# ScalarE's copies four slots behind TensorE's products in two tiles of an expert gather, with the query products and weight slots reordered

## What is computed

```python
def peer_ffn(h, wq, subkeys, u, v):
    ...
    q = (hf @ wq).reshape(T, PEER_HEADS, 2, D_HALF)
    s = jnp.einsum('thpd,pnd->thpn', q, subkeys, preferred_element_type=jnp.float32)
    top_s, top_i = lax.top_k(s, PEER_TOPK)
    cand = top_s[:, :, 0, :, None] + top_s[:, :, 1, None, :]
    best_s, best_j = lax.top_k(cand.reshape(T, PEER_HEADS, PEER_TOPK * PEER_TOPK), PEER_TOPK)
    ...
    expert = (i1 * N_KEYS + i2).reshape(T, PEER_HEADS * PEER_TOPK)
    gate = jax.nn.softmax(best_s, axis=-1).reshape(T, PEER_HEADS * PEER_TOPK).astype(h.dtype)
    ...
        uc = jnp.take(u, ec, axis=0)
        a = jnp.einsum('cd,ced->ce', hc, uc)
        act = jax.nn.gelu(a, approximate=False) * gc
        vc = jnp.take(v, ec, axis=0)
        return jnp.einsum('ce,ced->cd', act, vc)
```

## Time and profile before

| what | value |
|---|---|
| runs | 2619.51, 2631.34, 2619.8 us |
| median | 2619.8 us |
| span of the profiled execution, first to last instruction | 2623.7 us |
| PE / DVE / ACT / POOL busy | 81% / 51% / 30% / 40% of the span |
| tile 0 (window 170 to 556 us) | 386 us, 370 GB/s |
| tile 1 (556 to 990) | 434 us, 403 GB/s |
| tile 2 (990 to 1397) | 407 us, 368 GB/s |
| tile 3 (1397 to 1780) | 383 us, 371 GB/s |

### The profile page before, as it was taken

The page is one execution under the profiler, slowest core; times in us unless marked ns, Lnnn a source line. Parts: engine busy times, 40 slices in busy tenths (PEclk is TensorE's granted clock), DMA queues, the critical chain, the costliest instruction groups (busy, mean ns, idle before and its releaser), DMA issues. The chain is left out here.

```text
span 2623.7 us, 27482 instructions
## 1 busy us (share of the span) xinstructions
PE 2126.1 (81%) x8468; PEld 1120.2 (43%) x8468; DVE 1350.4 (51%) x2888; ACT 777.3 (30%) x2244; POOL 1040.3 (40%) x1107
## 2 busy tenths in 40 slices
PE   4887987676877879878877678868889998988997
PEld 2454543232333344434533223325645444655543
DVE  6756678774566475564685664432522223232222
ACT  2243332232324334353333334332410102321101
POOL 4036666576666556665556666650010000000000
PEclk9898989888988989999988889898889998988999
DMA  9749999999999999999999999993159996209996
GB/s 374 302 185 343 362 359 385 379 392 403 411 413 409 404 377 385 392 369 364 362 346 351 397 386 371 372 366 126 47 208 415 418 418 234 81 6 383 418 418 279
DMA packets 236992, 879.66 MB, mean 335 GB/s; under 512 B 23282, under 2 KB 29954, under 8 KB 214338
## 3 DMA queue, kind: packets, MB, share of 16 engines
q0 software_dynamic: 149488, 543.97, 54.1%
q1 hardware_dynamic: 87380, 334.23, 32.2%
HBM read 877.07 MB, written 1.05 MB: 335 GB/s over the span
## 5 line engine op out<-in xcount | busy, mean ns | idle before, releaser
L2212 DVE CUSTOM_DVE_ANT_0 arena<-arena,PS 128x1024 f32<-128x1024 f32 x512 | 625.0, 1221 | 484.6 <-DMA arena<-in_peer_u_dram,IDX 361.5
L933 POOL DMA_INDIRECT arena<-in_peer_v_dram,IDX x512 | 501.5, 979 | 423.0 <-PE PS L1531 233.8
L1531 PE MATMUL PS<-arena,JK 128*128 128x512 f32 x1024 | 526.5, 655 | 166.9 <-ACT JK L1089 96.3
L1531 PE MATMUL PS<-arena 128*128 128x512 f32 x1024 | 516.5, 643 | 147.2 <-issue 74.1
L930 POOL DMA_INDIRECT arena<-in_peer_u_dram,IDX x512 | 493.9, 965 | 308.8 <-issue 146.7
L1531 PEld LDWEIGHTS PS<-arena,JK 128*128 128x128 f32 x1024 | 201.5, 208 | 441.6 <-issue 393.9
L1531 PEld LDWEIGHTS PS<-arena 128*128 128x128 f32 x1024 | 197.9, 205 | 412.0 <-issue 382.4
L1076 ACT ACTIVATE ACTV<-DOT 128x1 f32<-128x1 f32 x512 | 102.0, 199 | 768.0 <-DVE DOT L2212 447.8
L1925 PE MATMUL PS<-arena,HT 128*64 128x256 f32 x2048 | 236.6, 384 | 19.8 <-DMA arena<-in_w_down_dram 13.3
L1925 PEld LDWEIGHTS PS<-arena,HT 128*64 128x64 f32 x2048 | 148.9, 137 | 98.4 <-DMA arena<-in_w_down_dram 22.8
L1084 ACT ACTIVATE GACT<-ACTV,GATE 128x1 f32<-128x1 f32 x512 | 150.8, 295 | 23.1 <-issue 2.8
(11 more groups left out here) (351 smaller groups left out, 1940.2 us busy)
## 6 DMA issues: line engine op xcount, KB each, us to landing
arena<-in_w_gate_dram SPq DMA_DIRECT2D x64, 1024.0 KB, 16.3
arena<-in_w_up_dram SPq DMA_DIRECT2D x64, 1024.0 KB, 18.4
arena<-in_w_down_dram SPq DMA_DIRECT2D x64, 1024.0 KB, 15.4
arena<-in_w_ada_dram SPq DMA_DIRECT2D x22, 2048.0 KB, 12.6
arena<-in_w_in_dram SPq DMA_DIRECT2D x11, 2048.0 KB, 17.9
arena<-in_peer_wq_dram SPq DMA_DIRECT2D x10, 2048.0 KB, 8.2
arena<-in_w_out_dram SPq DMA_DIRECT2D x6, 2048.0 KB, 10.1
arena<-in_peer_u_dram,IDX POOLq DMA_INDIRECT x512
```

The lines of the kernel that those rows point to most:

```text
L933: pool.indirect_dma_start(out=GV[b], out_offset=None, in_=v_rows, in_offset=off).then_inc(v_loaded[b], 16)
L1531: last = pe.matmul(PO[:, half, :], DIAG[n % DIAGS], GV[BUF[n]][:, half * 512:(half + 1) * 512], start=(j == 0), stop=False, skip_group_che ...
L2212: dve.tensor_tensor_reduce(GU[BUF[n]], GU[BUF[n]], HP[tt].rearrange("p b n -> p (b n)"), 1.0, 0.0, ALU.mult, ALU.add, DOT[:, s:s + 1]).the ...
```

## The change

The copies of ACT in tiles 0 and 2 (and the query copies of tile 3) move from one slot behind the product to four (`COPY`), PE's product with the subkeys from one or two slots behind the query product to five (`SCORE`), and ACT's copy of the scores from two or three to nine (`KEYED`). The tables move nearly all the steps of tile 2 and the query products and routing stages of tile 0:

- Tile 0: the query products start 4 to 9 slots later, the stages of (0, 2) at 41, 45, 49 and of (0, 3) at 53, 56, 59.
- Tile 2: four query products instead of five, at 20 (0, 3), 29 (0, 2), 99 (1, 0) and 109 (1, 1); the mixer's steps lie 3 to 20 slots later (the input products at 11, 14, 17, the attention's scores at 43, its output products at 76 and 83 instead of 60 and 63); three groups of routing stages instead of four.
- Tile 3: the product (1, 3) at 20 and the routing of (1, 1) at 5, 9, 13 come here from tile 2.
- The chunk ("wq", 1, 3) is loaded earlier and stays in its place until tile 3, so all the other chunks of that stretch share place 0. The order in which PE gives chunks back is therefore no longer that in which they are loaded, and `weight_chunks` counts it apart.
- Two buffers are placed elsewhere (`POOLT`, one part of `SS`), and POOL's transfers for the second block are issued at slot 52 of tile 3 instead of 40.

The loops of PE (`slots_beside_second_mixer` at L1610) and the second half of the `psum_jobs` hunk change by the same numbers as those shown, and are left out.

```diff
@@ -65,10 +65,11 @@
 LATE = (4, 5)
 BESIDE_TILE1 = (0, 1, 4, 5)
 
-WQ_AT = {10: (1, 0, 8), 19: (0, 2, 6), 31: (0, 3, 8), 41: (1, 1, 8), 51: (1, 2, 8), 67: (1, 3, 8)}
-ROUTE_AT = ([(0, 1, j) for j in (10, 13, 16)] + [(0, 2, j) for j in (37, 42, 47)] + [(0, 3, j) for j in (53, 57, 61)]
+COPY, SCORE, KEYED = 4, 5, 9
+WQ_AT = {14: (1, 0, 8), 26: (0, 2, 6), 36: (0, 3, 8), 48: (1, 1, 8), 60: (1, 2, 8), 72: (1, 3, 8)}
+ROUTE_AT = ([(0, 1, j) for j in (10, 13, 16)] + [(0, 2, j) for j in (41, 45, 49)] + [(0, 3, j) for j in (53, 56, 59)]
             + [(1, n // 3, 62 + 5 * n) for n in range(12)])
-GATES_AT = {16: 1, 47: 2, 61: 3, 117: 4}
+GATES_AT = {16: 1, 49: 2, 59: 3, 117: 4}
 
 SUM_AT = {(5 * n // 2 if n < 8 else 48 + 5 * (n - 8) // 2): n for n in range(24)}
 ADA_AT = {24: 0, 26: 1, 28: 2, 30: 3, 68: 4, 70: 5, 72: 6, 75: 7, 90: 8, 92: 9, 93: 10, 96: 11}
@@ -78,15 +79,16 @@
 FIRST_ROUTE_AT = {**{109 + 2 * n: (0, 0, n) for n in range(3)}, **{115 + 3 * n: (0, 1, n) for n in range(3)}}
 FIRST_GATES_AT = {114: 0, 122: 1}
 
-IN2_AT = {8: 0, 11: 1, 14: 2}
-OUT2_AT = {60: 0, 63: 1}
-NEXT_WQ_AT = {33: (0, 2, 4), 66: (0, 3, 4), 80: (1, 3, 4), 86: (1, 0, 4), 96: (1, 1, 4)}
-NEXT_ROUTE_AT = {**{45 + 2 * n: (0, 2, n) for n in range(3)}, **{78 + 2 * n: (0, 3, n) for n in range(3)},
-                 **{98 + 3 * n: (1, 0, n) for n in range(3)}, **{108 + 4 * n: (1, 1, n) for n in range(3)}}
-NEXT_GATES_AT = {49: 2, 82: 3, 104: 4, 116: 5}
-LAST_WQ_AT = {6: (1, 2, 8)}
-LAST_ROUTE_AT = {**{23 + 4 * n: (1, 2, n) for n in range(3)}, **{35 + 4 * n: (1, 3, n) for n in range(3)}}
-LAST_GATES_AT = {31: 6, 43: 7}
+IN2_AT = {11: 0, 14: 1, 17: 2}
+OUT2_AT = {76: 0, 83: 1}
+NEXT_WQ_AT = {20: (0, 3, 4), 29: (0, 2, 4), 99: (1, 0, 3), 109: (1, 1, 4)}
+NEXT_ROUTE_AT = {**{44 + 2 * n: (0, 2, n) for n in range(3)}, **{52 + 4 * n: (0, 3, n) for n in range(3)},
+                 **{113 + 3 * n: (1, 0, n) for n in range(3)}}
+NEXT_GATES_AT = {48: 2, 60: 3, 119: 4}
+LAST_WQ_AT = {6: (1, 2, 8), 20: (1, 3, 8)}
+LAST_ROUTE_AT = {**{5 + 4 * n: (1, 1, n) for n in range(3)}, **{25 + 4 * n: (1, 2, n) for n in range(3)},
+                 **{39 + 4 * n: (1, 3, n) for n in range(3)}}
+LAST_GATES_AT = {13: 5, 33: 6, 47: 7}
 REST_AT = 71
 QUERIES_AT = 80
 PIECES = 8
@@ -212,39 +214,39 @@
         if j - 2 in FIRST_WQ_DONE:
             add(("s", 1, *FIRST_WQ_DONE[j - 2]), "s", LATE)
     for j in range(SLOTS):
-        banks = BESIDE_TILE0 if j <= 76 else LATE
+        banks = BESIDE_TILE0 if j <= 94 else LATE
         if j == 6:
             halves("hT", 1, 1, banks)
         if j in IN2_AT:
             add(("in", 1, 1, IN2_AT[j]), "s", banks)
-        if j == 17:
+        if j == 24:
             add(("pool", 1, 1), "s", banks)
-        if j == 20:
+        if j == 29:
             add(("mix", 1, 1), "v", banks)
-        if j == 27:
...
@@ -334,8 +336,8 @@
     *[(("ada", 1, n), "v", n % 2 * 2) for n in range(4, 12)],
     (("out", 1, 0, 0), "p", 0), (("out", 1, 1, 0), "p", 2), (("wq", 1, 0, 0), "p", 0), (("wq", 1, 1, 0), "p", 2),
     (("in", 1, 0, 1), "p", 0), (("in", 1, 1, 1), "p", 2), (("in", 1, 2, 1), "p", 6),
-    (("wq", 1, 2, 0), "p", 0), (("out", 1, 0, 1), "p", 2), (("out", 1, 1, 1), "p", 0), (("wq", 1, 3), "p", 2),
-    (("wq", 1, 0, 1), "p", 0), (("wq", 1, 1, 1), "p", 2), (("wq", 1, 2, 1), "p", 0),
+    (("wq", 1, 2, 0), "p", 0), (("wq", 1, 3), "p", 2), (("out", 1, 0, 1), "p", 0), (("out", 1, 1, 1), "p", 0),
+    (("wq", 1, 0, 1), "p", 0), (("wq", 1, 1, 1), "p", 0), (("wq", 1, 2, 1), "p", 0),
 ]
 for _l in range(DEPTH):
     CHUNKS += [(("bin", _l, 3), "p", 0), (("bin", _l, 0), "p", 2), (("bin", _l, 1), "p", 1), (("bin", _l, 2), "p", 3),
@@ -349,12 +351,16 @@
 def weight_chunks():
 
 
-    chunks, count, last, kth = {}, {"v": 0, "p": 0}, {}, {}
+    given, nth = [name for name, _, _ in CHUNKS if name != ("wq", 1, NQ - 1)], {}
+    given.insert(given.index(("wq", 1, 2, 1)) + 1, ("wq", 1, NQ - 1))
+    users = {name: who for name, who, _ in CHUNKS}
+    for who in "vp":
+        nth.update({name: n for n, name in enumerate(name for name in given if users[name] == who)})
+    chunks, last, kth = {}, {}, {}
     for name, who, slot in CHUNKS:
         kth[slot] = kth.get(slot, 0) + 1
-        chunks[name] = (kth[slot], slot, who, count[who], last.get(slot))
+        chunks[name] = (kth[slot], slot, who, nth[name], last.get(slot))
         last[slot] = name
-        count[who] += 1
     return chunks
 
 
@@ -467,7 +473,7 @@
         QSQ = [[ap[:, 0:640] for ap in row] for row in S_A]
         S_A = [[parts(ap, NH) for ap in row] for row in S_A]
         PT_A = [[gv(7680, 1024), gv(8704, 1024)], [mod[:, 3584:4608], mod[:, 2560:3584]]]
-        POOLT = [[parts(ap[:, 0:512], 4) for ap in row] for row in PT_A]
+        POOLT = [[parts(ap[:, 0:512], 4) for ap in row] for row in (PT_A[0], [PT_A[1][0]] * TT)]
         PT_A = [[parts(ap, NH) for ap in row] for row in PT_A]
         SUBK = [parts(gv(10240, 256), 2), parts(mod[:, 4608:4864], 2)]
         MIXG = gv(10752, 1024)
@@ -478,7 +484,7 @@
         QTP = [mod[:, 10240:11264], mod[:, 2560:3584]]
         QTP = [[parts(ap[:, i * 512:(i + 1) * 512], 4) for i in range(2)] for ap in QTP]
         SS = [[[tt * 2048 + c * 512 for c in range(NQ)] for tt in range(TT)],
-              [[1536, 3584, 512, 6144], [6656, 7168, 7680, 8192]]]
+              [[1536, 3584, 512, 0], [6656, 7168, 7680, 8192]]]
         SS = [[[parts(mod[:, at:at + 512], 4) for at in row] for row in rows] for rows in SS]
         OH = gv(8704, 512).rearrange("p (h k c) -> p h k c", h=HQ, k=TOPK)
         CAND = parts(HR[:, 0, 0:512], HQ)
@@ -931,8 +937,8 @@
                         if PREV[n] is not None:
                             pool.wait_ge(expert_added, PREV[n] + 1)
                         pool.indirect_dma_start(out=GV[b], out_offset=None, in_=v_rows, in_offset=off).then_inc(v_loaded[b], 16)
-                        if l == DEPTH - 1 and tt == 1 and j == 40:
-                            arrived(pool, ("s", 1, 1, 2))
+                        if l == DEPTH - 1 and tt == 1 and j == 52:
+                            arrived(pool, ("s", 1, 1, 3))
                             params([(FINAL, row(final_norm_2, P))])
                             params_of_b(0)
 
@@ -1097,13 +1103,13 @@
                     slot_gate(l, 0, j)
                     if j - 1 == 5:
                         x_root(1)
-                    if j - 1 == 9:
+                    if j - COPY == 9:
                         transposed("h2T", l, 1)
                         h_to_psum(l, 1)
-                    if j - 1 in WQ_DONE:
-                        query(l, *WQ_DONE[j - 1])
-                    if j - 2 in WQ_DONE:
-                        keyed(l, *WQ_DONE[j - 2])
+                    if j - COPY in WQ_DONE:
+                        query(l, *WQ_DONE[j - COPY])
+                    if j - KEYED in WQ_DONE:
+                        keyed(l, *WQ_DONE[j - KEYED])
 
             def queries_of(l, tt):
                 copy_out(("fq", l, tt), FQT[:, :, tt * P:(tt + 1) * P], parts(bank(("fq", l, tt)), 4))
@@ -1153,34 +1159,34 @@
                 for j in range(SLOTS):
                     if j == 4:
                         x_root(1)
-                    if j == 23:
+                    if j == 25:
                         head_root(1)
-                    if j == 38:
+                    if j == 50:
                         head_exps(l, 1)
-                    if j == 56:
+                    if j == 68:
                         y_root(1)
-                    if j == 72:
+                    if j == 91:
                         x_root(1)
                     if j - 2 in NEXT_GATES_AT:
                         gate_exp(l, NEXT_GATES_AT[j - 2])
                     slot_gate(l, 0, j)
-                    if j - 1 == 6:
+                    if j - COPY == 6:
                         transposed("hT", l, 1)
-                    if j - 1 in IN2_AT:
-                        projected(l, 1, IN2_AT[j - 1])
-                    if j - 1 == 17:
+                    if j - COPY in IN2_AT:
+                        projected(l, 1, IN2_AT[j - COPY])
+                    if j - KEYED in NEXT_WQ_DONE:
+                        keyed(l, *NEXT_WQ_DONE[j - KEYED])
+                    if j - COPY in NEXT_WQ_DONE:
+                        query(l, *NEXT_WQ_DONE[j - COPY])
+                    if j - COPY == 24:
                         pooled(l, 1)
-                    if j - 1 == 27:
+                    if j - COPY == 33:
                         heads_transposed(l, 1)
-                    if j - 1 in NEXT_WQ_DONE:
-                        query(l, *NEXT_WQ_DONE[j - 1])
-                    if j - 3 in NEXT_WQ_DONE:
-                        keyed(l, *NEXT_WQ_DONE[j - 3])
-                    if j - 1 == 42:
+                    if j - COPY == 54:
                         probs_transposed(l, 1)
-                    if j - 1 == 58:
+                    if j - COPY == 71:
```

(36 more changed lines are left out.)

43 lines of the change are left out of this document (22 added, 21 removed).

## The result

The changed kernel takes 2641.8 us (median of 20 runs, 2629.2 to 2652.0), the kernel before 2631.0 us (median of 20, 2608.5 to 2648.7). The ratio is 1.0043, with a 95% interval of 1.0026 to 1.0059: slower by 0.3 to 0.6%. The middle, 0.43%, lies just under the 0.5% that the prediction took as no change, but the interval excludes 1. Forecast were 14 us less. The three runs known at first had a median of 2619.8 us, 11 us low; the forecast sum, a difference, isn't touched by that. It had the wrong sign.

What follows compares the result with a forecast made beforehand. The gathers set the pace, held in tile 2 by PE's late adds. Terms -17 - 6 + 5 + 5 - 2 + 1 = -14 us gave 2606 us against the median 2619.8; range 2582 to 2637, likeliest case 2590 to 2612.

Steps and rivals of the forecast that it cites:

- Copies four slots later: Tile 2: later copies end ACT's waits and PE's gaps, so POOL's four holds go; -17 us, bounds 0 and -20.4.
- the four holds of the earlier trace: POOL's waits in tile 2 after PE's two gaps: first pair 3.69 and 4.72 us, second pair 7.78 and 5.43.
- the sign that the prediction itself had named: The prediction's main step is wrong if ACT's waits go and POOL's holds stay.
- rival A: The delay sits in PE's product count; later copies only move the wait, gaining about 5; 2618 us, chance 0.29.
- Product and routing leave tile 2: One query product and one routing group leave tile 2, relieving PE and DVE; -6 us, bounds 0 and -11.4.
- The same in tile 3: Routing of (1, 1) and product (1, 3) crowd the start of tile 3; +5 us, bounds 0 and +13.
- Stages closer together: Routing stages crowd DVE in tile 0 (+2) and in slots 44 to 60 of tile 2 (+3); +5 us.
- Tile 0's copies: Tile 0: a hold behind slot 10 shrinks (-4), scores copied just ahead of stages cost +2; -2 us.
- The chunk places: Chunk (1, 3) may land late, 0 to 3 us of PE; later chunks hidden by 7 slots; +1 us.
- rival B: DVE's crowded stages hold the gathers, up to 20 us in tile 2, 13 in tile 3; 2639 us, chance 0.20.
- The rule that spoke against a gain: About 358 GB/s limits a core's HBM share, so tile 2 could not gain: sum 0, 2620 us.

Runs made afterwards that it cites:

- e3: The changed kernel with ACT's copies back at one slot behind the product (COPY = 1), score distances left changed; ratio to the kernel before 1.0031.
- e11: e10 with ACT's copies back at one slot behind the product (COPY = 1); ratio to the kernel before 0.9961.
- e1: The kernel before with only tile 0's part of the change, tiles 1 to 3 as they were; ratio to the kernel before 1.0007.
- e12: The kernel before with tile 2's output products at slots 63 and 65 instead of 60 and 63; ratio to the kernel before 1.0001.
- e8: The changed kernel with tile 2's product (0, 2) first and its routing stages at 33, 38, 41, ahead of the softmax; ratio to the kernel before 0.9978.
- e10: The changed kernel with tile 0 as before, e8's tables and e6's output slot; 2610.9 us, ratio to the kernel before 0.9942.
- e7: The kernel before with only the routing stages of (1, 1) moved from tile 2 to slots 5, 9, 13 of tile 3; ratio 0.9992.
- e2: The changed kernel with tile 0 put back as it was, tiles 2 and 3 left changed; ratio to the kernel before 1.0040.
- e6: The changed kernel with tile 2's second output product at slot 87 instead of 83; ratio to the kernel before 1.0008.
- e5: The changed kernel with tile 2's routing stages of (0, 3) back at slots 78, 80 and 82; ratio to the kernel before 1.0033.
- e9: The changed kernel with tile 0's first query product in four parts instead of eight; ratio to the kernel before 1.0005.
- e4: The changed kernel with copies, scores and score copies back at one, two and three slots, tables left changed; ratio to the kernel before 1.0018.

## Why the prediction was wrong

- **Copies four slots later, -17.** This is the step that failed. That ACT stands before the copies, and that later copies end it, was right (57.7 us of "remote" to 11.2). That the four holds of the earlier trace rows come from these waits was not: ACT's waits shrank and POOL's holds stayed, the sign that the prediction itself had named. I read an order in time (PE's gap, then POOL's hold) as a cause. e3 brings 52 us of ACT's waits back at no cost, and e11 bounds the term at 13 us with 5 as its middle. Of the holds, the second pair stands in e1 with hardly a wait of ACT ahead of it, and the first pair, 8.4 of the 21.6 us, didn't recur in e1 and e12. What the traces show in place of it is the wait itself, wherever it stands, as in rival A, and A's gain of 5 us fits: where ACT doesn't meet the delay of PE's counts, PE does, in its own wait behind the product, 8.29 us in e1 and 11.1 to 11.6 us in e8, e10 and e11, with the copies at one slot and at four alike. That this delay makes the holds is read from where they stand, eight slots behind the product; no run removed it, so it isn't shown as their cause. The products are besides 14 us of PE's own work in a few slots, and PE wins back only 2.48 - 1.88 = 0.6 us in each free one.
- **Product and routing leave tile 2, -6.** Not measured alone. e7, the routing part of it with its other end in tile 3, gave -2 us, within its interval of -8 to +4, and a tile 2 that was 7 to 10 us shorter.
- **The same in tile 3, +5.** e7 says no net cost for the routing. Nor does the longer tile 3 of the changed kernel, 389.6 us, say otherwise: e2 and e6 have the same tables there and took 381.3 and 384.0 us.
- **Stages closer together, +5.** Mis-sized, and its place misread. I took 3 for tile 2 because six stages crowd in slots 44 to 60. By e5 the three later ones cost nothing that can be measured, by e8 the three earlier ones with the softmax cost 7 to 9 us of holds; the 13 to 17 us by which e8 is faster are more than that and not all explained. The tables that I counted from listed only routing stages; `scored` at slot 49 is in the diff.
- **Tile 0's copies, -2.** The holds behind slot 10 did shrink, but a wait was missed. The change moved the release of ("wq", 0, 0) past slot 24, where a gather takes that place: 6.4 to 7.6 us more in every kernel with the product at 14 to 21. e9 takes it away. What it costs isn't shown, since the holds around it sum to no more than before's; the whole of tile 0's part is -3 to +7 us by e1, which doesn't exclude the forecast.
- **The chunk places, +1.** For (1, 3) it was right: PE waited 1.95 us for it at slot 20. But the later ones were to be covered by 7 slots, 17.4 us; the second output chunk took 19.7 us from its issue to the product, and PE waited 7.23 us, since its issue itself came only when the first product, late and 10.12 us long, was through. In e3, e4 and e8, where the first product was on time, the wait was absent. e6 puts it at 3 to 5 us by its ratio, unproved, and at 8 to 12 by tile 2.

With what the runs show in place of the terms, 0 to -5 for the copies, -2 for what e7 moves, +7 to +9 for the crowded slots, -3 to +7 for tile 0 and +3 to +5 for the chunk, the sum is 0 to +19 us; measured were +10.8 and, from 1.0026, +6.8. So wide a sum only shows that nothing large is missing. The outcome is rival A in what the copies are worth and half of rival B in what the tables cost. B's price of 20 us in tile 2 was too high, and of its 13 us in tile 3 e7 shows nothing. That the range, 2582 to 2637 us, missed 2641.8 is in part chance: it was laid around a median of three runs that was 11 us low.

The rule that spoke against a gain fell as it stood there: tile 2 of e10 ran at 387 GB/s for 380.7 us, where 368 stood before. The Trainium skill, page "DMA: Bandwidth & Descriptors", section Bandwidth, says itself that the 358 GB/s hold when both cores of a domain stream and that a core alone was measured at up to 425; one core ran here, and the trace agrees (400 to 403 GB/s over the whole of tile 1).

## What to carry to other kernels

An idle engine ahead of a late one isn't its cause: before pricing a wait, ask whether the hold behind it would move with the work. The cheapest test is another profile of the same instructions, as e1's tile 2: where the wait is short by chance, is the hold gone? To shift the work instead of removing the wait, as e12 does, tests it too, but it shifts the weights' loads with it. When steps of a hand-written order are moved, list for each engine everything that stands in the new slots, and for each buffer who takes its place next and in which slot; the crowded slots and the late chunk were of these kinds and could be read from the code. And before the length of a stretch is explained, take several profiles of it: here identical instructions took 389 to 404 us in tile 0, but 398 to 402 us in the changed tile 2.

## What the hardware showed beside this

The same instructions of tile 0, with the same waits, lasted 389.0 us in one execution and 404.1 us in another, and the runs of before spread over 40 us or 1.5%, far more than the 0.3% named at the start. DVE idled 3.13 us ("remote") inside a routing stage, before a cast that waits for nothing but DVE's own step before it: the stage of slot 44 takes 11.0 us from dot to dot, and this is its longest wait. The stages of the earlier trace rows show the same: 12.5 and 14.6 us from dot to dot for 6.5 us of work. A DMA share near 1 isn't yet the highest rate: tile 2 moved 366 GB/s at a share of 0.96, tile 1 of before 403 GB/s at 1.02, 10% more for 6%. Why PE's own count came up to 11.6 us behind the recorded end of a product, no run tells.
